# Output projection of a hybrid attention layer: eight column-and-token products replaced by seven half-size products

## The chip, the cores and the metric

The kernel runs on one core of a Trainium2 chip. The time is device microseconds of one execution; before the change it is 531.4 us (median of three runs, 531.16 to 531.54). Lower is better.

## The reference

One layer takes `x` (1024 tokens by 1024 features, float32), normalises it, projects it with `w_in`, runs two groups of attention heads, gates both, and projects the concatenated mix back:

```
h = rmsnorm(x, pre_g);  p = h @ w_in
ya = sliding_window_sink_attention(...) * silu(ag)     # 512 mix features
yb = differential_attention(...) * silu(bg)            # 512 mix features
y = concat([ya, yb]) @ w_out                           # (1024 x 1024) @ (1024 x 1024)
return x + rmsnorm(y, post_g)
```

The change concerns the product with `w_out` and what surrounds it. The norm after it is over a whole row of 1024 columns: a token's scale is known only when all of its columns are.

## The kernel before

The engines are programmed by hand, each with its own instruction list, and they meet only in semaphores. One list of steps, `SCHEDULE`, is built by `make_schedule()`; every engine walks it and issues its own part of each step, so the order of steps sets the order on every engine.

A float32 product is made at full matmul rate by splitting both operands into a high part in the fp32r format and a low part, the rest; three products high-high, low-high and high-low (`PASSES`) are added up in PSUM. ScalarE (ACT) makes a high part with a Copy; VectorE (DVE) or GpSimd (POOL) makes the low part with a subtraction of two SBUF tensors.

The input projection goes in 21 units (`UNITS`) of two halves, cut into six pieces of 4 matmuls; the pieces are spread between the steps of attention. The last five units are gates: ACT takes a tanh of PSUM (L775), DVE multiplies with PSUM (L973) and then with the head's output (L980), which lies in `qT_A` for group A and `out_B` for group B. After the last attention block some 20 pieces remain, and between them the steps `split_out` (wo_hi on ACT L744, wo_lo on POOL L660 for even k and DVE L984 for odd k) and `y_split` stand. SyncE issues the loads of `w_out` row block by row block (L584) into freed buffers.

The output projection runs over eight tiles of 128 tokens (t) and two column halves. One (t, half) is 24 matmuls of 128x512 (8 blocks of k in 3 passes, L1263) into one of four PSUM banks in `scores`. After it ACT squares the bank with a row sum (L851), DVE weights it with post_g (L1087), and when both halves of a tile are done DVE adds the sums (L1084), POOL takes the power -0.5 (L626), DVE scales and adds x (L1094, two instructions), and ACT issues the two stores (L858). The y parts of tile t+2 are split (ACT L841, DVE L1071) while tile t is multiplied. Each tile so finishes behind its own matmuls.

## Time and profile before

| | |
|---|---|
| median of 3 runs | 531.4 us |
| span of the profiled execution | 529.6 us |
| median minus span | 1.8 us |
| PE busy | 511.7 us, 97% |
| DVE, ACT, POOL busy | 269.9, 250.5, 105.8 us |
| output projection, from first matmul to the last | 436.25 to 523.97 us |
| from there to the end of the span | 5.6 us |

The span counts from the first to the last instruction of one execution. The profile gives no total of its own for that execution; the median is 1.8 us above its span. PE matmul spans overlap each other in the profile, so the distance between the starts of two rows, and not their lengths, gives the pace of the matmuls.

### The profile page before, as it was taken

How to read it: one execution, taken by the hardware profiler on the slowest of the kernel's cores; microseconds unless marked ns; L12 is line 12 of the kernel's file. 1: busy time of each engine (PE TensorE's matmuls, PEld its weight loads, DVE VectorE, ACT ScalarE, POOL GpSimd, SP SyncE). 2: the span in 40 equal slices, each digit the busy share in tenths (PEclk: the TensorE clock that was granted, in tenths of full speed). 3: DMA queues.
4: the chain of work that ended last, by engine and by line, in shares of the span. 5: the costliest groups of instructions: out<-in, count | busy, mean ns of one | idle time of the engine just before them, and what ended most of it. 6: DMA issues, size and time to landing. Idle time of an engine off the chain costs nothing.

```text
span 529.6 us, 7514 instructions
## 1 busy us (share of the span) xinstructions
PE 511.7 (97%) x2776; PEld 424.8 (80%) x2776; DVE 269.9 (51%) x650; ACT 250.5 (47%) x614; POOL 105.8 (20%) x91
## 2 busy tenths in 40 slices
...
GB/s 295 228 123 2 1 15 143 41 74 6 40 10 33 40 41 0 41 40 9 34 41 27 14 41 1 40 41 41 0 1 0 144 176 120 102 132 84 80 79 79
DMA packets 41300, 32.57 MB, mean 61 GB/s; under 512 B 18544, under 2 KB 35888, under 8 KB 41264
## 3 DMA queue, kind: packets, MB, share of 16 engines
...
q14 instruction: 14, 0.11, 0.1%
HBM read 27.40 MB, written 4.19 MB: 60 GB/s over the span
## 4 chain that ended last, share of the span: by engine, by line
PE 85%; ACT 4%; DVE 4%; issue 3%; DMA 2%; POOL 2%; SPq 0%; DVEq 0%; POOLq 0%; ACTq 0%
PE proj L1164 39%; PE scores L1263 14%; PE proj L1134 10%; PE scores L1183 7%; PE banks L1204 6%; PE banks L1194 3%; PE scores L1228 2%; PE banks L1246 2%; PE banks L1236 1%; PE scores L1107 1%; DVE k_stack L961 1%; DMA pre_g<-in_pre_norm_g 1%; DMA w_raw<-in_w_in 1%; ACT k_stack L762 1%; PE banks L1213 1%
## 5 line engine op out<-in xcount | busy, mean ns | idle before, releaser
L1164 PE MATMUL proj<-hT_hi,w_hi 128*128 128x512 f32 x336 | 90.0, 401 | 0.8 <-DVE k_stack L961 0.6
L1164 PE MATMUL proj<-hT_lo,w_hi 128*128 128x512 f32 x336 | 90.6, 402 | 0.0
L622 POOL TENSOR_TENSOR w_lo<-w_raw,w_hi 128x1024 fp32r<-128x1024 f32 x21 | 51.0, 2430 | 195.4 <-ACT w_hi L711 195.4
L1164 PE MATMUL proj<-hT_hi,w_lo 128*128 128x512 f32 x336 | 89.2, 400 | 0.0
L1164 PEld LDWEIGHTS proj<-hT_hi,w_hi 128*128 128x128 f32 x336 | 60.3, 188 | 15.0 <-issue 1.9
L1164 PEld LDWEIGHTS proj<-hT_hi,w_lo 128*128 128x128 f32 x336 | 60.8, 188 | 13.7 <-issue 1.9
L1164 PEld LDWEIGHTS proj<-hT_lo,w_hi 128*128 128x128 f32 x336 | 59.9, 188 | 13.2 <-issue 1.9
L1016 DVE CUSTOM_DVE_ANT_0 weights<-scores,dist_b 128x128 f32<-128x128 f32 (+7 forms) x64 | 45.9, 755 | 47.2 <-PE scores L1183 47.0
L782 ACT ACTIVATE weights<-weights,small 128x128 f32<-128x128 f32 (+7 forms) x64 | 49.0, 767 | 14.0 <-DVE small L1016 14.0
L792 ACT ACTIVATE weightsT<-banks 128x512 f32<-128x512 f32 (+3 forms) x48 | 23.5, 490 | 51.4 <-PE banks L1194 51.4
L1183 PE MATMUL scores<-k_stack,q_stack 128*128 128x512 f32 (+3 forms) x192 | 41.9, 353 | 0.0
L1204 PEld LDWEIGHTS banks<-v_sb,weightsT 128*128 128x128 f32 x288 | 36.3, 191 | 5.8 <-ACT weightsT L792 3.2
L1204 PE MATMUL banks<-v_sb,weightsT 128*128 128x128 f32 x288 | 37.8, 276 | 1.1 <-ACT weightsT L792 1.1
L1183 PEld LDWEIGHTS scores<-k_stack,q_stack 128*128 128x128 f32 x192 | 31.9, 189 | 4.8 <-DVE k_stack L961 0.4
L1000 DVE SCALAR_TENSOR_TENSOR weights<-weights,small,weights 128x512 f32<-128x512 f32 (+3 forms) x48 | 34.4, 745 | 1.1
L851 ACT ACTIVATE banks<-scores 128x512 f32<-128x512 f32 x16 | 9.3, 582 | 53.3 <-PE scores L1263 53.3
L626 POOL TENSOR_TENSOR small<-small 128x1 f32<-128x1 f32 (+1 forms) x24 | 16.9, 704 | 82.7 <-DVE small L1084 81.4
L1263 PE MATMUL scores<-wo_hi,hT_hi 128*128 128x512 f32 x128 | 32.0, 391 | 0.1
L820 ACT ACTIVATE a_weights<-a_weights,small 128x128 f32<-128x128 f32 x64 | 24.9, 391 | 14.7 <-DVE small L1044 14.6
L1263 PE MATMUL scores<-wo_hi,hT_lo 128*128 128x512 f32 x128 | 31.6, 389 | 0.0
L1263 PE MATMUL scores<-wo_lo,hT_hi 128*128 128x512 f32 x128 | 31.6, 389 | 0.0
L961 DVE TENSOR_TENSOR k_stack<-proj,k_stack 64x512 fp32r<-64x512 f32 x32 | 22.0, 688 | 15.6 <-ACT k_stack L762 14.8
...
## 6 DMA issues: line engine op xcount, KB each, us to landing
...
```

Source lines behind the costliest of these rows:

```text
L622: nc.gpsimd.tensor_tensor(w_lo[:, n % SPLIT], w_raw[:, n % RAW], w_hi[:, n % SPLIT].bitcast(F32), ALU.subtract).then_inc(w_lo_ready, 1)
L782: nc.scalar.activation(w, w, ACT.Exp, scale=-1.0, bias=min_b[:, 2 * u + m:2 * u + m + 1], accum_out=sum_b[:, 2 * u + m:2 * u + m + 1]).the ...
L792: nc.scalar.activation(weightsT[:, 4 * r:4 * r + blocks, :], turned[:, 0:P * blocks].rearrange("p (b q) -> p b q", q=P), ACT.Copy).then_in ...
L820: nc.scalar.activation(w, w, ACT.Exp, scale=-1.0, bias=min_a[:, s + j:s + j + 1], accum_out=sum_a[:, s + j:s + j + 1]).then_inc(a_exped, 1)
L961: nc.vector.tensor_tensor(k_lo[part, m, tokens], source[own, :], k_hi[own, m, tokens].bitcast(F32), ALU.subtract).then_inc(stack_lo, 1)
L1000: nc.vector.scalar_tensor_tensor(w0, w1, mix_b[:, u:u + 1], w0, ALU.mult, ALU.add).then_inc(b_mixed, 1)
L1016: nc.vector.tensor_tensor_reduce(out=weights_1[:, 0:keys] if m else weights_0[:, u % 2, 0:keys], in0=scores[:, 1024 * m:1024 * m + keys], ...
L1134: last = nc.tensor.matmul(proj[:, n % 2, 0:VG], h[:, k, tokens], w[:, k, cols], start=(p == 0 and k == 0), stop=(p == PASSES - 1 and k == ...
L1164: last = nc.tensor.matmul(to, w[:, slot, k, :], h[:, k, HALF * half:HALF * half + HALF], start=(p == 0 and k == first), stop=(p == PIECES ...
L1183: last = nc.tensor.matmul(scores[:, 1024 * m + first:1024 * m + first + width], q_stack[head][m][:, P * block_:P * block_ + P], k[:, m, fi ...
L1204: last = nc.tensor.matmul(mixed[:, P * (u % 4):P * (u % 4) + P], weightsT[:, b, :], v_sb[:, b, P * head:P * head + P], start=(b == 0), sto ...
L1263: last = nc.tensor.matmul(scores[:, at:at + HALF], y[:, k, tokens], w[:, k, cols], start=(p == 0 and k == 0), stop=(p == PASSES - 1 and k ...
```

## The change

The 1024x1024x1024 product is cut into halves of tokens, of mix features and of columns: y = [A1 B1; A2 B2] (tokens 0 to 511 and 512 to 1023; group A and group B features) and w_out = [W00 W01; W10 W11]. Instead of eight half-size products, seven are made, each 512 tokens by 512 features by 512 columns, that is four PSUM banks of 12 matmuls of 128x512 (4 blocks of k in 3 passes): 48 matmuls. Their operands and results:

- T1 = W01-W00, T2 = W11-T1, T4 = W10-T2, T3 = W11-W01 on POOL (step `wo_sums`), 2048 elements per partition each; S1 = A2+B2, S2 = S1-A1, S3 = A1-A2, S4 = B1-S2 on DVE (`y_sum`), two instructions of 1024 elements each.
- in this order: P1 = A1·W00 and P2 = B1·W10, P6 = S2·T2, P7 = S3·T3, P5 = S1·T1, P3 = S4·W11, P4 = B2·T4. P6, P7 and P4 go on top of P1 in the four banks of `scores`; P2 has the two `banks` and the two `proj`, and then P5 starts there and P3 goes on top.
- running sums are taken out between products: ACT copies `scores` after P1, P6 and P7 (`u_copied`), DVE adds the other four banks to these copies after P2, P5 and P3 (`c_added`). Each next product waits in each bank for the copy or add of that bank.

All operands are split again into high and low parts: ACT makes wo_hi (2048 elements in one instruction) and y_hi (two of 1024) for every product, DVE makes y_lo (two of 1024) for every product and wo_lo for P1 and P2, POOL makes wo_lo for the other five. They live in three sets of buffers (`OUT_SLOTS`), so product i waits with its splits for the end of product i-3. `w_out` is loaded as a whole, 4 MB, into one buffer when the last attention product is done.

Squares of each half row (ACT) follow the adds. The rest of the tiles' ends, for all eight tiles, now stands in DVE's list behind the adds of P3, that is behind everything else, and all stores stand in ACT's list behind the last squares.

The core of the diff (declarations, index functions, buffer places left out; P1 ... P4 are numbers 0 to 6 in the order P1, P2, P6, P7, P5, P3, P4):

```diff
-    for t in range(TILES):
-        if t + 2 < TILES:
-            steps.append(("y_split", t + 2))
-        steps += [("out_project", t, 0), ("out_project", t, 1), ("post", t)]
+        if len(pieces) - at == WO_HIGH_AT:
+            steps.append(("wo_split", P1))
+        if len(pieces) - at == 9:
+            steps.append(("y_split", P1))
+    steps += [("y_split", P2), ("wo_split", P2), ("wo_sums",)]
+    steps += [("out_product", P1), ("y_sum", SUM_S1), ("y_sum", SUM_S2), ("y_split", P6), ("wo_split", P6)]
+    steps += [("out_product", P2), ("y_sum", SUM_S3), ("y_split", P7), ("wo_split", P7)]
+    steps += [("out_product", P6), ("y_sum", SUM_S4), ("y_split", P5), ("wo_split", P5)]
+    steps += [("out_product", P7), ("y_split", P3), ("wo_split", P3)]
+    steps += [("out_product", P5), ("y_split", P4), ("wo_split", P4)]
+    steps += [("out_product", P3), ("out_product", P4)]
...
+            sp.wait_ge(b_valued, B_UNITS)
+            for side in range(2):
+                rows = w_out[0, A_PAIRS * HEAD_DIM * side:A_PAIRS * HEAD_DIM * (side + 1), :]
+                sp.dma_start(wo_raw[HEAD_DIM * side:HEAD_DIM * (side + 1), 0:HALF_K, :],
+                             rows.rearrange("(k p) d -> p k d", p=HEAD_DIM)).then_inc(wo_loaded[0], 16)
+            for k, head in enumerate(B_ORDER):
+                sp.dma_start(wo_raw[:, HALF_K + k, :],
+                             w_out[0, A_WIDTH + P * head:A_WIDTH + P * head + P, :]).then_inc(wo_loaded[1], 16)
...
+                elif step == "wo_sums":
+                    pool.wait_ge(wo_loaded[1], 64)
+                    pool.wait_ge(wo_lo_ready, P1 + 1)
+                    nc.gpsimd.tensor_tensor(wo_part(0, 0), wo_part(0, 1), wo_part(0, 0),
+                                            ALU.subtract).then_inc(wo_summed, 1)
+                    pool.wait_ge(w_lo_ready, NU)
+                    pool.wait_ge(projected, 2 * NU)
+                    pool.wait_ge(wo_summed, DIF_T1)
+                    nc.gpsimd.tensor_tensor(t2[:, :, :], wo_part(1, 1), wo_part(0, 0),
+                                            ALU.subtract).then_inc(wo_summed, 1)
+                    pool.wait_ge(wo_summed, DIF_T2)
+                    pool.wait_ge(wo_lo_ready, P2 + 1)
+                    nc.gpsimd.tensor_tensor(wo_part(1, 0), wo_part(1, 0), t2[:, :, :],
+                                            ALU.subtract).then_inc(wo_summed, 1)
+                    nc.gpsimd.tensor_tensor(wo_part(0, 1), wo_part(1, 1), wo_part(0, 1),
+                                            ALU.subtract).then_inc(wo_summed, 1)
+                elif step == "wo_split" and i[0] > P2:
+                    n = i[0]
+                    pool.wait_ge(wo_hi_ready, n + 1)
+                    nc.gpsimd.tensor_tensor(wo_lo[n % OUT_SLOTS][:, :, :], wo_operand(n),
+                                            wo_hi[n % OUT_SLOTS][:, :, :].bitcast(F32),
+                                            ALU.subtract).then_inc(wo_lo_ready, 1)
...
+                    elif n == P4:
+                        dve.wait_ge(post_g_loaded, 16)
+                        low, high = slice(0, HALF), slice(HALF, D_MODEL)
+                        for t in range(TILES):
+                            early, late = ((0, low), (1, high)) if t < PAIRS else ((1, high), (0, low))
+                            for half, cols in (early, late):
+                                dve.wait_ge(y_squared, squares_done(t, half))
+                                if half == late[0]:
+                                    nc.vector.scalar_tensor_tensor(
+                                        y_mean[:, t:t + 1], y_square[:, 2 * t:2 * t + 1], EPS,
+                                        y_square[:, 2 * t + 1:2 * t + 2], ALU.add, ALU.add).then_inc(y_meaned, 1)
+                                c = c_half(t, half)
+                                weighted = c11[:, t % PAIRS, :] if t >= PAIRS and half == 0 else c
+                                if t >= PAIRS and half == 0:
+                                    dve.wait_ge(y_added, 2 * (t - PAIRS) + 2)
+                                nc.vector.tensor_tensor(weighted, c, post_g[:, cols],
+                                                        ALU.mult).then_inc(y_weighted, 1)
+                            dve.wait_ge(y_weighted, 2 * t + 2)
+                            dve.wait_ge(res_loaded[t], 16)
+                            dve.wait_ge(y_rooted, t + 1)
...
+                elif step == "out_product":
+                    n = i[0]
+                    slot = n % OUT_SLOTS
+                    for r in range(PAIRS):
...
+                        elif n in (P6, P7, P4):
+                            pe.wait_ge(u_copied, PAIRS * {P6: 0, P7: 1, P4: 2}[n] + r + 1)
...
+                        for p, (y, w) in enumerate(((y_hi, wo_hi), (y_lo, wo_hi), (y_hi, wo_lo))):
+                            if r == 0 and p == 0:
+                                pe.wait_ge(wo_hi_ready, n + 1)
+                            if r == 0 and p == 2:
+                                pe.wait_ge(wo_lo_ready, n + 1)
```

How instructions stand on POOL before, from the first split of `w_out` to the last root (`wo_lo` is the low part of the weights, `small` a tile's column sum):

```order
L660 TENSOR_TENSOR wo_lo<-wo_early,wo_hi 128x1024
L660 TENSOR_TENSOR wo_lo<-w_raw,wo_hi 128x1024
L660 TENSOR_TENSOR wo_lo<-wo_early,wo_hi 128x1024
L660 TENSOR_TENSOR wo_lo<-w_raw,wo_hi 128x1024
L626 TENSOR_TENSOR small<-small 128x1 x8
```

POOL's part is over before the first tile's end; behind it stand only the roots.

The same place on POOL in the changed kernel (`wo_raw` is all of w_out, `t_101` is T2, `wo_lo_90` to `92` are the low parts in the three buffer sets):

```order
L714 TENSOR_TENSOR wo_raw<-wo_raw 128x4x512
L719 TENSOR_TENSOR t_101<-wo_raw 128x2048
L723 TENSOR_TENSOR wo_raw<-wo_raw,t_101 128x4x512
L725 TENSOR_TENSOR wo_raw<-wo_raw 128x4x512
L730 TENSOR_TENSOR wo_lo_92<-t_101,wo_hi_89 128x2048
L730 TENSOR_TENSOR wo_lo_90<-wo_raw,wo_hi_87 128x2048
L730 TENSOR_TENSOR wo_lo_91<-wo_raw,wo_hi_88 128x2048
L730 TENSOR_TENSOR wo_lo_92<-wo_raw,wo_hi_89 128x2048
L730 TENSOR_TENSOR wo_lo_90<-wo_raw,wo_hi_87 128x2048
L679 TENSOR_TENSOR small<-small 128x1 x8
```

Four instructions of 1024 elements have become nine of 2048, the four sums in front of the first wo_lo.

DVE before, at the start of the output projection (`hT_lo` is the low part of y, `hT_hi` the high part; `y_out` is a tile's weighted result):

```order
L973 SCALAR_TENSOR_TENSOR gate<-gate,proj 128x512
L980 TENSOR_TENSOR out_B<-gate,out_B 128x512
L1071 TENSOR_TENSOR hT_lo<-qT_A,hT_hi 128x2x128 x2
L1071 TENSOR_TENSOR hT_lo<-out_B,hT_hi 128x4x128
L1087 TENSOR_TENSOR y_out<-scores,post_g 128x512
L1084 SCALAR_TENSOR_TENSOR small<-small 128x1
L1087 TENSOR_TENSOR y_out<-scores,post_g 128x512
L1094 SCALAR_TENSOR_TENSOR y_out<-y_out,small,x_res 128x512 x2
```

The split of the next tile, two or three instructions of at most 512 elements, stands in front of the end of the current one; each tile repeats that.

DVE in the changed kernel at the same place, from the last gate's product to the splits for P7 (`s_99` is S1, `s_100` S2, `y_lo_96` to `98` low parts of y, `c_103` the sums of tokens 0 to 511, columns 0 to 511):

```order
L1073 SCALAR_TENSOR_TENSOR gate<-gate,proj 128x512
L1080 TENSOR_TENSOR out_B<-gate,out_B 128x512
L1171 TENSOR_TENSOR y_lo_97<-out_B,y_hi_94 128x1024 x2
L1084 TENSOR_TENSOR wo_lo_91<-wo_raw,wo_hi_88 128x2048
L1184 TENSOR_TENSOR s_99<-qT_A,out_B 128x1024 x2
L1188 TENSOR_TENSOR s_100<-s_99,qT_A 128x1024 x2
L1171 TENSOR_TENSOR y_lo_98<-s_100,y_hi_95 128x1024 x2
L1203 TENSOR_TENSOR c_103<-banks,c_103 128x512 x2
L1203 TENSOR_TENSOR c_103<-proj,c_103 128x512 x2
L1191 TENSOR_TENSOR qT_A<-qT_A 128x2x8x64 x2
L1171 TENSOR_TENSOR y_lo_96<-qT_A,y_hi_93 128x1024 x2
```

The end of a tile no longer stands between the splits; sums and splits of two SBUF tensors stand in a row there.

DVE in the changed kernel behind the adds of P3 (`c_102` are the sums of tokens 0 to 511, columns 512 to 1023; `x_res` a tile of x, which becomes the output):

```order
L1203 TENSOR_TENSOR c_102<-banks,c_102 128x512 x2
L1203 TENSOR_TENSOR c_102<-proj,c_102 128x512 x2
L1219 TENSOR_TENSOR c_103<-c_103,post_g 128x512
L1212 SCALAR_TENSOR_TENSOR small<-small 128x1
L1219 TENSOR_TENSOR c_102<-c_102,post_g 128x512
L1226 SCALAR_TENSOR_TENSOR x_res_107<-c_103,small,x_res_107 128x512
L1226 SCALAR_TENSOR_TENSOR x_res_107<-c_102,small,x_res_107 128x512
```

Before, such a group of five stood behind each tile's matmuls; now the eight groups stand in a row, of which the first is shown.

## Rows read from the trace of the kernel before

**Rows 1.** The page: busy time of each engine.

```profile
span 529.6 us, 7514 instructions
...
PE 511.7 (97%) x2776; PEld 424.8 (80%) x2776; DVE 269.9 (51%) x650; ACT 250.5 (47%) x614; POOL 105.8 (20%) x91
```

**Rows 2.** The chain that ended last, from 380 us: start, length, engine, tile, line.

```profile
409.55 1.87 PE banks L1204 x16
...
438.20 74.90 PE scores L1263 x329
```

**Rows 3.** Timeline of PE, output projection: start, length, engine, line, operation.

```profile
436.25 2.45 PE L1263 MATMUL scores<-wo_hi,hT_hi 128*128 128x512 f32 x8
438.53 2.01 PE L1263 MATMUL scores<-wo_hi,hT_lo 128*128 128x512 f32 x8
440.38 1.98 PE L1263 MATMUL scores<-wo_lo,hT_hi 128*128 128x512 f32 x8
...
521.99 1.98 PE L1263 MATMUL scores<-wo_lo,hT_hi 128*128 128x512 f32 x8
```

**Rows 4.** Timeline of all engines, the last tile.

```profile
519.35 0.69 DVE L1087 TENSOR_TENSOR y_out<-scores,post_g 128x512 f32<-128x512 f32 x1 [3.17 <-ACT banks L851]
...
524.00 0.58 ACT L851 ACTIVATE banks<-scores 128x512 f32<-128x512 f32 x1 [4.75 <-PE scores L1263]
524.49 0.19 ACT L851 ACTIVATION_READ_ACCUMULATOR banks<-scores 128x1 f32 x1
524.72 0.16 DVE L1084 SCALAR_TENSOR_TENSOR small<-small 128x1 f32<-128x1 f32 x1 [4.68 <-ACT banks L851]
524.80 0.68 DVE L1087 TENSOR_TENSOR y_out<-scores,post_g 128x512 f32<-128x512 f32 x1
524.96 0.55 POOL L626 TENSOR_TENSOR small<-small 128x1 f32<-128x1 f32 x1 [10.33 <-DVE small L1084]
525.64 1.41 DVE L1094 SCALAR_TENSOR_TENSOR y_out<-y_out,small,x_res 128x512 f32<-128x512 f32 x2 [0.16 <-POOL small L626]
526.42 1.00 ACTq L858 DMA_DIRECT2D out<-y_out  x2
```

**Rows 5.** Timeline, 418 to 445 us: ACT, POOL and DVE split weights.

```profile
420.62 2.00 ACT L744 ACTIVATE wo_hi<-wo_early 128x1024 fp32r<-128x1024 f32 x2
...
425.57 0.60 ACT L775 ACTIVATE gate<-proj 128x512 f32<-128x512 f32 x1 [2.94 <-PE proj L1164]
...
427.19 2.69 POOL L660 TENSOR_TENSOR wo_lo<-w_raw,wo_hi 128x1024 fp32r<-128x1024 f32 x1 [2.75 <-ACT wo_hi L744]
...
428.09 2.87 DVE L984 TENSOR_TENSOR wo_lo<-w_raw,wo_hi 128x1024 fp32r<-128x1024 f32 x1 [0.48 <-ACT wo_hi L744]
...
429.84 3.38 POOL L660 TENSOR_TENSOR wo_lo<-wo_early,wo_hi 128x1024 fp32r<-128x1024 f32 x1
...
431.01 0.60 ACT L775 ACTIVATE gate<-proj 128x512 f32<-128x512 f32 x1 [2.00 <-PE proj L1164]
...
433.69 1.21 DVE L984 TENSOR_TENSOR wo_lo<-wo_early,wo_hi 128x1024 fp32r<-128x1024 f32 x1
...
437.28 2.45 POOL L660 TENSOR_TENSOR wo_lo<-w_raw,wo_hi 128x1024 fp32r<-128x1024 f32 x1 [4.06 <-ACT wo_hi L744]
```

**Rows 6.** Timeline, 110 to 118 us: DVE reading PSUM beside POOL.

```profile
113.76 2.39 POOL L622 TENSOR_TENSOR w_lo<-w_raw,w_hi 128x1024 fp32r<-128x1024 f32 x1 [4.83 <-ACT w_hi L711]
113.85 1.41 DVE L956 SCALAR_TENSOR_TENSOR q_stack<-proj,q_stack 64x512 fp32r<-64x512 f32 x2
```

**Rows 7.** Timeline of the DMA queue of SyncE, loads of w_out.

```profile
414.21 2.45 SPq L584 DMA_DIRECT2D wo_early<-in_w_out  x4
416.78 2.78 SPq L584 DMA_DIRECT2D w_raw<-in_w_out  x4
```

**Rows 8.** Stretches: us, busy of PE, PEld, DVE, ACT, POOL, clock, DMA share, GB/s.

```profile
415.00:420.00 5.00, 5.00 (x26) 4.12 (x25) 1.96 (x3) 0.69 (x1) 0.00 (x0) 1.00 0.93 206
420.00:430.00 10.00, 10.00 (x46) 8.29 (x45) 7.53 (x6) 5.94 (x7) 5.50 (x3) 1.00 0.79 212
```

**Rows 9.** Stretches after the last matmul (PEclk is the granted clock).

```profile
524.00:526.00 2.00, 0.00 (x0) 0.00 (x0) 1.12 (x3) 0.69 (x2) 0.55 (x1) 1.00 0.00 0
526.00:527.00 1.00, 0.00 (x0) 0.00 (x0) 1.00 (x2) 0.00 (x0) 0.00 (x0) 0.72 0.00 0
527.00:528.00 1.00, 0.00 (x0) 0.00 (x0) 0.05 (x1) 0.00 (x0) 0.00 (x0) 0.50 0.74 272
```

**Rows 10.** Timeline of PE at the start.

```profile
1.54 5.38 PE L1140 MATMUL proj<-ident 128*128 128x128 f32 x24 [1.54 <-POOL ident L631]
...
18.39 1.06 PE L1107 MATMUL scores<-ident,x_in 128*128 128x128 f32 x8 [1.00 <-DVE x_in L869]
```

**Rows 11.** Groups by shape, POOL: busy, mean ns, idle before.

```profile
L622 POOL TENSOR_TENSOR w_lo<-w_raw,w_hi 128x1024 fp32r<-128x1024 f32 x21 | 51.0, 2430 | 195.4 <-ACT w_hi L711 195.4
...
L643 POOL TENSOR_TENSOR wv_lo<-wv_raw,wv_hi 128x1280 fp32r<-128x1280 f32 x1 | 2.9, 2927 | 3.7 <-ACT wv_hi L686 3.7
```

**Rows 12.** Groups by shape, ACT.

```profile
L792 ACT ACTIVATE weightsT<-banks 128x512 f32<-128x512 f32 x24 | 14.3, 596 | 21.6 <-PE banks L1194 21.6
...
L744 ACT ACTIVATE wo_hi<-wo_early 128x1024 fp32r<-128x1024 f32 x4 | 4.1, 1054 | 0.0
```

More of the change, by code:

```diff
@@ L76 @@
 WV_AT = 5
-Y_PARTS = 3
-WO_RAW = 4
-OLDEST = NU % SPLIT
 FIRST_PIECES = 24
+PAIRS = TILES // 2
+HALF_K = KT // 2
+PRODUCTS = 7
+P1, P2, P6, P7, P5, P3, P4 = range(PRODUCTS)
+Y_ORIGINALS = {P1: (0, 0), P2: (1, 0), P4: (1, 1)}
+SUM_S1, SUM_S2, SUM_S3, SUM_S4 = range(1, 5)
+DIF_T1, DIF_T2, DIF_T4, DIF_T3 = range(1, 5)
+OUT_SLOTS = 3
 B_UNITS = B_HEADS * TILES
@@ L202, in make_schedule @@
         take(max(0, count))
-    last = (NU - 1) * 2 * PIECES
-    outs = list(range(KT))
     while at < len(pieces):
@@ L275, in hybrid_layer @@
     lam_in = place("lam_in", 118, [P, 4, HEAD_DIM])
-    wo_hi = place("wo_hi", 96, [P, KT, D_MODEL], F32R)
-    wo_lo = place("wo_lo", 128, [P, KT, D_MODEL], F32R)
-    wo_early = place("wo_early", 72, [P, 2 * SPLIT, D_MODEL])
-    post_g = place("post_g", 201.75, [P, D_MODEL])
-    x_res = place("x_res", 76, [P, 2, D_MODEL])
-    y_out = place("y_out", 88, [P, 2, D_MODEL])
+    wo_raw = place("wo_raw", 96, [P, KT, D_MODEL])
+    out_slots = [128, 0, 32]
+    wo_hi = [place(f"wo_hi{i}", at, [P, HALF_K, HALF], F32R) for i, at in enumerate(out_slots)]
+    wo_lo = [place(f"wo_lo{i}", at + 8, [P, HALF_K, HALF], F32R) for i, at in enumerate(out_slots)]
+    y_hi = [place(f"y_hi{i}", at + 16, [P, HALF_K, HALF], F32R) for i, at in enumerate(out_slots)]
+    y_lo = [place(f"y_lo{i}", at + 24, [P, HALF_K, HALF], F32R) for i, at in enumerate(out_slots)]
+    s1 = place("s1", 64, [P, HALF_K, HALF])
+    s2 = place("s2", 72, [P, HALF_K, HALF])
+    t2 = place("t2", 80, [P, HALF_K, HALF])
+    c12 = place("c12", 80, [P, PAIRS, HALF])
+    c11 = place("c11", 88, [P, PAIRS, HALF])
+    c22_parts = [place("c22_low", 180.25, [P, 2, HALF]), place("c22_high", 188.25, [P, 2, HALF])]
+    post_g = place("post_g", 160.25, [P, D_MODEL])
+    x_res = [place(f"x_res{t}", (64 if t < PAIRS else 96) + 4 * (t % PAIRS), [P, D_MODEL]) for t in range(TILES)]
     taken = [0]
@@ L328, in hybrid_layer @@
     mixed = banks[:, 512:1024]
+    out_x = [scores[:, HALF * r:HALF * r + HALF] for r in range(PAIRS)]
+    out_y = [turned, mixed, proj[:, 0, :], proj[:, 1, :]]
     def sem(name):
@@ L335, in hybrid_layer @@
     w_loaded = [sem(f"w_loaded{i}") for i in range(RAW)]
-    wo_loaded = [sem(f"wo_loaded{i}") for i in range(WO_RAW)]
+    wo_loaded = [sem("wo_loaded0"), sem("wo_loaded1")]
     pre_g_loaded = sem("pre_g_loaded")
@@ L340, in hybrid_layer @@
     v_shifted = sem("v_shifted")
-    res_loaded = [sem("res_loaded0"), sem("res_loaded1")]
-    stored = [sem("stored0"), sem("stored1")]
+    res_loaded = [sem(f"res_loaded{t}") for t in range(TILES)]
+    stored = sem("stored")
     ident_made = sem("ident_made")
@@ new lines, in heads_b, with half_rows, y_operand @@
+    def heads_b(half, r):
+        tokens = out_B[:, 2 * r:2 * r + 2, HALF * half:HALF * half + HALF]
+        return tokens.rearrange("p s (c q) -> p s c q", q=CHUNK)
+    def half_rows(to, r):
+        return to[:, 2 * r:2 * r + 2, :].rearrange("p s (c q) -> p s c q", q=CHUNK)
+    def y_operand(i, r):
+        if i in Y_ORIGINALS:
+            side, half = Y_ORIGINALS[i]
+            return heads_b(half, r) if side else heads_a(half, r)
+        if i == P7:
+            return heads_a(1, r)
+        return half_rows(s1 if i == P5 else s2, r)
@@ new lines, in wo_part, with wo_operand, c22, c_half @@
+    def wo_part(rows, cols):
+        return wo_raw[:, HALF_K * rows:HALF_K * (rows + 1), HALF * cols:HALF * cols + HALF]
+    def wo_operand(i):
+        if i == P6:
+            return t2[:, :, :]
+        return wo_part(*{P1: (0, 0), P2: (1, 0), P7: (0, 1), P5: (0, 0), P3: (1, 1), P4: (1, 0)}[i])
+    def c22(r):
+        return c22_parts[r // 2][:, r % 2, :]
+    def c_half(t, half):
+        r = t % PAIRS
+        if t < PAIRS:
+            return (c12 if half else c11)[:, r, :]
+        return c22(r) if half else out_x[r]
```

306 lines of the change are left out of this document (167 added, 139 removed).

## The prediction

> **What bounds the kernel now.** I read the page first: PE is busy 97% of a span of 529.6 us, every other engine half of it or less [rows 1]. Then the chain of waits: its last long piece is 74.9 us of output-projection matmuls in one run [rows 2]. The PE timeline gives their pace: groups of 8 start at 440.38 and, 45 groups later, at 521.99, so one matmul takes 81.61/360 = 0.2267 us. The first two groups start 2.28 and 1.85 us after one another's beginning instead of 1.81: some 0.5 us is lost at the start [rows 3]. Last I read the end: the last product ends at 523.97, ACT squares, DVE sums and weights, POOL makes the root, DVE scales, the stores go out, and the span ends 5.6 us after PE [rows 4]. PE sets the time, and a tile's end is hidden behind the next tile's matmuls for all tiles but one.
>
> The span is 1.8 us below the median of the runs. I sum over the span and add 1.8 at the end.
>
> **Matmuls.** 16 groups of 24, or 384, become 7 x 4 x 12 = 336. 48 x 0.2267 = 10.9 us go. The operands of P1 are ready early: ACT's wo_hi starts behind the gate of 425.57 [rows 5], y_hi is done near 430.2, DVE's low parts near 432.9, and PE needs them at 436.25. So the 0.5 us goes too: -11.4 us. Copies and adds that free a bank have a product's time, 10.9 us, for four of about 0.6 to 0.7 us [rows 4, 12]: nothing, as long as their engines are not late.
>
> **The tiles' ends.** DVE gets all eight behind the adds of P3. One costs 0.69 for the first weighting, then from 524.72 to 527.05 for sum, second weighting, root and two scalings [rows 4]: 3.02 us, eight are 24.2 us. From the end of P3 it takes 0.04 + 0.7 (its last add) + 24.2 to the last scaling, and the stores another 2.55 (527.05 to 529.6) [rows 1, 4]. In tiles 0 to 3 the second weighting now reads two SBUF tensors and POOL's root may stand behind it (below): 0 to 0.45 us each, I take half, 0.9 in all. That is 28.4 us from the end of P3. P4 lies beside the first 10.9 of them, 17.5 are left after PE. Before, 5.6: +11.9 us. ACT's twelve later squares at 0.77 [rows 4] and the x loads lie beside this. The tail alone eats what the matmuls give.
>
> **The port between DVE and POOL.** The rows show one rule. A POOL instruction of 427.19 ends at 429.88; DVE's of 428.09 ends at 430.96, 1.08 later; POOL's next, issued at 429.84, ends at 433.22, 2.26 after DVE; alone they take 1.21 and 2.43 [rows 5, 11]. So they ran in turns, neither beside the other, and the one that waited went first, even between two POOL instructions in a row. DVE's with one operand in PSUM ran 1.41 for two beside POOL, undisturbed [rows 6]. The Trainium skill, SBUF — State Buffer, "Who interferes with whom", has this as a rule that speaks against the change: a DVE instruction with two SBUF inputs contends with a GpSimd instruction that reads SBUF, and the one that issues second blocks fully. By that rule, the trace agrees, the 11.3 us below are owed; without it the sum would be that of rival 1.
>
> The change puts nine 2048-element instructions on POOL where four of 1024 stood, beside sums and splits of two SBUF tensors on DVE. Their price: POOL 2.43 + 2.27 = 4.7 us (from 1024 to 1280 elements it rose 0.5 us, which would give 4.4; twice 2.43 gives 4.86) [rows 11]. The Trainium skill, GPSIMD Engine Reference, "Elementwise — side-by-side cycle accounting", states 4497 ns for this size; no row here has it, and by that figure the wait below would be about 0.8 us shorter. DVE 1.2 for 1024, 2.3 for 2048 [rows 5]. ACT 1.05 for 1024, 1.95 for 2048 (+0.9 per 1024 by 596 against 1054) [rows 12].
>
> The list, step by step. The last attention product ends at 411.42 [rows 2]; w_out's 4.19 MB flow at 206 to 268 GB/s (212 at a share of 0.79) [rows 8], so the rows of P1 are in by about 423 and all by 429 to 434, with the 2 us that issues take [rows 7]. T1 starts near 432 and runs to 437.4 (behind one DVE instruction), and the last but one gate product on DVE waits for it; T2 follows to 442.5, and the last gate product waits too. y_lo of P2 twice and wo_lo of P2 then end at 447.8; PE wants wo_lo of P2 at 447.1 + 1.8 = 448.9: hidden with 1 us to spare. From there it isn't. POOL has T4 (it waits for wo_lo of P2) and T3, DVE has S1, S1, S2, S2, and they take turns: S1 449.0, T4 453.6, S1 454.6, T3 459.2, S2 460.3, S2 461.5. Behind S2 stands ACT with y_hi of P6 (463.6) and, in its list behind that, wo_hi of P6 (465.6), though T2 was ready long before. PE ends P2 at 458.0 and waits 7.6 us. POOL makes wo_lo of P6 from 465.6 to 470.3; PE's third pass is there at 467.4 and waits 3.0. For P7 the same pair costs 0.7, since S3 stands behind POOL too. P5, P3 and P4 find their operands ready: the work per product there is one POOL instruction and at most six on DVE in 10.9 us. Sum of the waits: +11.3 us.
>
> **The clock.** PE idle from 523.97 had its full 2.4 GHz until 526 and half of it in the slices from 526 and 527 (0.72, 0.50) [rows 9]. At the start 24 small transposes took 5.38 us, 0.22 each, later 8 took 1.06, about 0.13 [rows 10]. So after 7.6 us without work P6 starts at 1.2 GHz. Half of some 6 us, 3.0, is the upper end; zero if it comes back while PE waits for wo_lo. The first 8 matmuls at half speed end just before 470.3 and are free; I take 1.2.
>
> Sum: 529.6 - 11.4 + 11.9 + 11.3 + 1.2 = 542.6 us of span; with 1.8, **544.4 us**, 2.4% slower.
>
> **Bounds.** POOL's size: four of its instructions stand on the way to P6, -1.2 to +0.6. Clock -1.2 to +1.8. Root -0.9 to +0.9. Loads: if all of w_out is in only at 438, +4. Turns: if DVE kept the port through its row of four, S2 would be done by 452.6, but T4, T3 and wo_lo then follow in a row and P6 still gets its low part near 469: about the same.
>
> **Rivals.** 1. No turn is lost at the port, DVE and POOL run beside each other. For: in all of the run before the port cost the path nothing one can see. Against: the three pairs in rows 5. Then POOL needs five times 4.7 from 432, is done with wo_lo of P6 at 455.5, before 459.8, and PE never waits: 529.6 - 11.4 + 11.0 (no root wait) = 529.2, with 1.8 531.0, no difference.
> 2. Faster, by the length of a tile's end on DVE. With the port free the time is 531.0 + 8 x (t - 3.02) for t us a tile, and it is faster by 0.2% from t below 2.94. It could be 2.7, 528.4 us, if DVE overlapped its instructions where no sum or root is fresh (the squares of tiles 0 to 3 are old when it starts). Against: 2.33 of the 3.02 are one chain in rows 4, which the new list keeps whole for each tile, and rows 5 say that the port isn't free.
> 3. The port costs only part (an ACT list that gets y_hi of P6 out early, or smaller POOL instructions): half of 11.3, 537 to 538.
> 4. It costs more: w_out late, waits at P2 too, half clock through P6 and again at P7: 549 to 555. For: PE has 1 us of slack at P2.
>
> **How the numbers follow.** Forecast 0.68, rival 1 0.08, rival 2 0.04, rival 3 0.09, rival 4 0.11. The forecast's own bounds give 541 to 549. The range of 8 in 10 takes a part of rivals 3 and 4: 538 to 551. What a measurement can tell from no change is 0.2%, 530.3 to 532.5. Faster: rival 2 and a quarter of rival 1, which a little rounding carries below 530.3: 0.06. Same: most of the rest of rival 1, 0.05. Slower 0.89.
>
> **What would show it.** In the profile after: PE groups at the same 0.2267; gaps before the first matmul of P6 of 7 to 8 us, after a group of 8 in it some 3 us, near 0.7 in P7, none before P5, P3, P4; DVE S1 and S2 rows of 5.6 us in place of 1.2, beside POOL's of 4.7; a granted clock under 1 around 460 to 470 us; and behind the last matmul a row of DVE instructions of 15 us with PE idle. I am wrong if DVE's two-SBUF instructions keep 1.2 us beside POOL, if PE's end is before 515, or if DVE's last scaling comes under 10 us after PE's end.

## The result and the profile after

The changed kernel takes 542.77 us (median of 4 runs, 542.50 to 544.03), the kernel before on the same chip 531.44: ratio 1.0216, 95% interval 1.0202 to 1.0229. 544.4 us was forecast, 1.6 us or 0.3% too much. The profiled execution of the changed kernel was its slowest, 544.03 us; a later series of the same kernel, whose profiled execution took 542.43 us, serves beside it below and is called the second profile.

The page of the changed kernel: span, busy time of PE, DVE and POOL, PE in 40 slices and its granted clock.

```profile
span 542.2 us, 7425 instructions
PE 504.8 (93%) x2728; PEld 418.4 (77%) x2728; DVE 312.5 (58%) x658; ACT 266.2 (49%) x615; POOL 141.1 (26%) x96
PE   6899999999999999999898999999999997599970
PEclk9999999999999999999999999999999999599995
```

PE had 511.7 us to do over 529.6 and has 504.8 over 542.2 [rows 1]: it has less work and more idle time. The holes stand in two places, slices 34 and 35 (about 447 to 474 us) and the last two. In slice 35 and in the last one the granted clock is 0.5, half of full speed.

PE's timeline in the output projection (start, duration, groups of matmuls; the brackets tell the idle time before and what ended it): the first group, the first of P6, its second and third pass, and the last of the program.

```profile
436.13 1.07 PE L1409 MATMUL scores<-wo_hi,y_hi 128*128 128x512 f32 x4
465.92 2.05 PE L1409 MATMUL scores<-wo_hi,y_hi 128*128 128x512 f32 x4 [7.84 <-ACT wo_hi L819]
470.51 2.07 PE L1409 MATMUL scores<-wo_lo,y_hi 128*128 128x512 f32 x4 [0.84 <-POOL wo_lo L730]
524.50 1.07 PE L1409 MATMUL scores<-wo_lo,y_hi 128*128 128x512 f32 x4
```

P1 starts where the first tile did [rows 3]. P1 and P2 are 96 matmuls of 0.2267 us and end at 457.9; P6 starts at 465.92, 8.0 us later. The third pass stands 4.59 us behind it, where 8 matmuls at full clock take 1.81. Here they ran at half clock, 3.7 us, and then PE waited the rest for POOL's low part; at full clock the wait would be 2.8.

What stood in front of P6 on DVE, POOL and ACT (three views, DVE's from 430 us on):

```profile
430.10 6.76 DVE L1171 TENSOR_TENSOR y_lo<-qT_A,y_hi 128x1024 fp32r<-128x1024 f32 x2
437.49 4.39 DVE L1080 TENSOR_TENSOR out_B<-gate,out_B 128x512 f32<-128x512 f32 x1
448.52 6.75 DVE L1184 TENSOR_TENSOR s<-qT_A,out_B 128x1024 f32<-128x1024 f32 x2
455.20 6.72 DVE L1188 TENSOR_TENSOR s<-s,qT_A 128x1024 f32<-128x1024 f32 x2
```
```profile
448.75 5.45 POOL L723 TENSOR_TENSOR wo_raw<-wo_raw,t 128x2048 f32<-128x2048 f32 x1 [7.41 <-DVE wo_lo L1084]
454.16 5.54 POOL L725 TENSOR_TENSOR wo_raw<-wo_raw 128x2048 f32<-128x2048 f32 x1
465.89 4.56 POOL L730 TENSOR_TENSOR wo_lo<-t,wo_hi 128x2048 fp32r<-128x2048 f32 x1 [6.19 <-ACT wo_hi L819]
```
```profile
462.01 2.00 ACT L918 ACTIVATE y_hi<-s 128x1024 fp32r<-128x1024 f32 x2 [13.79 <-DVE s L1188]
463.92 1.89 ACT L819 ACTIVATE wo_hi<-t 128x2048 fp32r<-128x2048 f32 x1
```

S1 and S2, two instructions of 1.2 us each, took 6.75 and 6.72 where 2.4 would do; T4 and T3 stood beside them at 5.45 and 5.54, where one that nothing disturbs (wo_lo of P6) takes 4.56. A blocked instruction is drawn longer, not as idle time. The same happened earlier: T1 (430.32 to 435.77) held y_lo of P1, T2 (436.43 to 441.34) a gate product of 0.69 us, drawn as 4.39. ACT had been idle for 13.8 us, waiting for S2, with wo_hi of P6 behind y_hi in its list.

The end, all engines, behind the last matmul, which ends at 525.57: the root of tile 3, the first weightings of tiles 4 and 5, then of tile 7 the second weighting, the root and the two scalings.

```profile
525.88 0.93 POOL L679 TENSOR_TENSOR small<-small 128x1 f32<-128x1 f32 x1 [2.30 <-DVE small L1212]
528.27 0.69 DVE L1219 TENSOR_TENSOR c_low<-c_low,post_g 128x512 f32<-128x512 f32 x1
531.12 0.68 DVE L1219 TENSOR_TENSOR c_low<-c_low,post_g 128x512 f32<-128x512 f32 x1
537.48 0.68 DVE L1219 TENSOR_TENSOR c<-scores,post_g 128x512 f32<-128x512 f32 x1
537.64 0.55 POOL L679 TENSOR_TENSOR small<-small 128x1 f32<-128x1 f32 x1 [2.30 <-DVE small L1212]
538.33 0.75 DVE L1226 SCALAR_TENSOR_TENSOR x_res<-c,small,x_res 128x512 f32<-128x512 f32 x1 [0.16 <-POOL small L679]
539.00 0.75 DVE L1226 SCALAR_TENSOR_TENSOR x_res<-c_high,small,x_res 128x512 f32<-128x512 f32 x1
```

PE ends at 525.57, DVE's last scaling at 539.75, the span at 542.2: 16.6 us behind PE, where the kernel before had 5.6 [rows 4].

### The profile page after: what moved, and what is told of

It reads as the page before. It is cut to its first block, busy times and chain, and to the rows that moved or that the text cites. A ratio compares the mean times of both kernels' runs of the same rounds, so it can differ in the third digit from the quotient of the medians.

```text
span 542.2 us, 7425 instructions
## 1 busy us (share of the span) xinstructions
PE 504.8 (93%) x2728; PEld 418.4 (77%) x2728; DVE 312.5 (58%) x658; ACT 266.2 (49%) x615; POOL 141.1 (26%) x96
## 4 chain that ended last, share of the span: by engine, by line
PE 76%; DVE 10%; ACT 4%; POOL 3%; issue 3%; DMA 2%; SPq 0%; DVEq 0%; POOLq 0%; ACTq 0%
PE proj L1296 37%; PE proj L1266 10%; PE scores L1315 6%; PE banks L1336 6%; PE scores L1409 4%; PE banks L1326 3%; PE proj L1409 2%; PE banks L1409 2%; DVE x_res L1226 2%; PE scores L1360 2%; PE banks L1378 2%; DVE s L1184 1%; DVE s L1188 1%; POOL small L679 1%; PE banks L1368 1%
## 5 line engine op out<-in xcount | busy, mean ns | idle before, releaser
L1145 DVE CUSTOM_DVE_ANT_0 a_weights<-scores,dist_a,small 128x128 f32<-128x128 f32 x64 | 22.5, 407 | 13.6 <-PE scores L1360 13.5
L747 POOL TENSOR_TENSOR a_weights<-a_weights,small 128x512 f32<-128x512 f32 x16 | 16.6, 1041 | 39.2 <-DVE small L1159 39.2
L1409 PE MATMUL scores<-wo_hi,y_hi 128*128 128x512 f32 x64 | 18.9, 421 | 7.8 <-ACT wo_hi L819 7.8
L1326 PE MATMUL banks<-ident,weights 128*128 128x128 f32 x144 | 23.8, 274 | 2.3 <-ACT weightsT L868 1.6
L851 ACT ACTIVATE gate<-proj 128x512 f32<-128x512 f32 x16 | 9.5, 592 | 33.3 <-PE proj L1296 22.8
```

The lines of the kernel that those rows point to most:

```text
L1326: last = nc.tensor.transpose(turned[:, P * (b - 4 * r):P * (b - 4 * r) + P], weights_0[:, u % 2, P * b:P * b + P], ident[:, :])
L1409: last = nc.tensor.matmul(to, y[slot][:, k, P * r:P * r + P], w[slot][:, k, :], start=(starts and p == 0 and k == 0), stop=(p == PASSES - ...
```

## Why it came so: two costs, four terms

My theory after this comparison is the prediction's: the tile ends behind the last product, and turns at the port that DVE and POOL share, each cost about what the matmuls give. Against it stand three rivals: that something else about the new sums holds P6 up (ACT's list, the loads, DVE's load as such); that a long tail is owed to the eight ends as such and can't be moved; and that half clock is a third cost of its own.

### The port: take POOL's sums away

```diff
-  nc.gpsimd.tensor_tensor(wo_part(0, 0), wo_part(0, 1), wo_part(0, 0), ALU.subtract)
+  nc.gpsimd.tensor_tensor(wo_part(0, 0)[:, :, 0:8], wo_part(0, 1)[:, :, 0:8], wo_part(0, 0)[:, :, 0:8], ALU.subtract)
```

(the same for T2, T4 and T3; P6 takes W11 as its second operand. The kernel leaves out nearly all of the four sums.)

> The four sums of w_out on POOL compute 8 of each 512 columns, and P6 takes W11 for T2: the kernel leaves out nearly all of T1 to T4. Theory (POOL's long instructions hold the port, and DVE's sums of two SBUF tensors wait for them): DVE's S1 and S2 take about 1.2 us each, P6 and P7 start on time, the granted clock stays full, the whole 13.1 us before P4's end come back: 529.7 us. Rival (the wait before P6 is the length of ACT's and DVE's own lists, without the port): DVE and ACT do the same work, so most of the 8 us before P6 stays: about 538.

531.37 us (10 runs, 530.89 to 531.64), ratio to before 0.9993 (0.9983 to 1.0002). DVE's rows of S1 and S2 and, later, of S4 in this kernel:

```profile
443.04 2.41 DVE L1184 TENSOR_TENSOR s<-qT_A,out_B 128x1024 f32<-128x1024 f32 x2
445.37 2.41 DVE L1188 TENSOR_TENSOR s<-s,qT_A 128x1024 f32<-128x1024 f32 x2
464.68 6.77 DVE L1194 TENSOR_TENSOR s<-out_B,s 128x1024 f32<-128x1024 f32 x2
```

S1 and S2 are back at 1.2 each, PE's timeline has no gap from P1 to the last product, and 11.4 us come back; the tail is still 16.7. The rival's 538 is out. The 529.7 that I gave was 1.7 too low: it counted the 13.1 us between P2 and P4 of the first profile, with its half clock (below). The time is near that of the prediction's rival 1, 531.0. S1 also starts 5.5 us earlier than in the changed kernel (443.04 against 448.52), since T1 and T2 no longer hold DVE before it. S4 beside POOL's wo_lo of P7 still took 6.77 in this kernel: the port goes on costing, but there it lies behind PE's work. This kernel takes two causes away at once, POOL's time for the sums and the turns; the next one parts them.

### The port: take away only DVE's second operand in SBUF

```diff
+  dve.wait_ge(u_copied, PAIRS)
-  nc.vector.tensor_tensor(half_rows(s1, r), heads_a(1, r), heads_b(1, r), ALU.add)
+  nc.vector.tensor_tensor(half_rows(s1, r), psum_rows(r), heads_b(1, r), ALU.add)
-  nc.vector.tensor_tensor(half_rows(s2, r), half_rows(s1, r), heads_a(0, r), ALU.subtract)
+  nc.vector.tensor_tensor(half_rows(s2, r), psum_rows(r), heads_a(0, r), ALU.subtract)
```

> S1 and S2 on DVE read their first operand from PSUM (the bank of P1) in place of SBUF, so the sums are of other data; sizes, order and all of POOL's work stay, and DVE waits in addition for ACT's copies of P1. Theory (only a DVE instruction with two SBUF operands is kept out by POOL): S1 and S2 take 1.2 us each beside T4 and T3, S2 is done near 453.5, P6 starts on time, and then waits some 5 us for its second y_lo (which has two SBUF operands and stands behind T3 and wo_lo of P6), and P7 some 3 us: 3 to 4 us less than the changed kernel in all, about 539.3 us. Rival (POOL slows every DVE instruction, or DVE's time is its own): no change, 542.8.

539.29 us (538.92 to 539.69), ratio 1.0144 (1.0129 to 1.0159), 3.5 us under the changed kernel. DVE from S1 to y_lo of P6, and POOL beside it:

```profile
448.84 2.35 DVE L1189 TENSOR_TENSOR s<-scores,out_B 128x1024 f32<-128x1024 f32 x2
451.11 2.35 DVE L1193 TENSOR_TENSOR s<-scores,qT_A 128x1024 f32<-128x1024 f32 x2
454.64 10.18 DVE L1175 TENSOR_TENSOR y_lo<-s,y_hi 128x1024 fp32r<-128x1024 f32 x2 [1.19 <-ACT y_hi L922]
```
```profile
449.07 4.63 POOL L727 TENSOR_TENSOR wo_raw<-wo_raw,t 128x2048 f32<-128x2048 f32 x1 [7.41 <-DVE wo_lo L1088]
453.66 4.62 POOL L729 TENSOR_TENSOR wo_raw<-wo_raw 128x2048 f32<-128x2048 f32 x1
458.25 5.49 POOL L734 TENSOR_TENSOR wo_lo<-t,wo_hi 128x2048 fp32r<-128x2048 f32 x1
```

With one operand in PSUM the same sums take 1.2 us each beside POOL's T4, and T4 takes 4.63: neither feels the other. The Trainium skill, SBUF — State Buffer, "Who interferes with whom", says that a DVE instruction with at most one SBUF input, outside the 2-port perf modes, does not contend with GpSimd; by that rule, the trace agrees. The next pair with two operands in SBUF, y_lo of P6, pays instead: 10.18 us for two, the first behind T3, the second behind wo_lo of P6. On PE:

```profile
459.42 0.73 PE L1414 MATMUL scores<-wo_hi,y_lo 128*128 128x512 f32 x2
464.88 1.22 PE L1414 MATMUL scores<-wo_hi,y_lo 128*128 128x512 f32 x2 [4.72 <-DVE y_lo L1175]
```

P6 starts without a wait, and 5.0 us go in its second pass (two matmuls from 459.42 end their turn at 459.87, the next start at 464.88), where the changed kernel waits 8.0 and 2.8. With 0.3 us for the first y_lo and 0.8 before P7's third pass, the waits are 6.1 us against 11.1. That they did not bring 5.0 us but 3.5 is half clock behind the pause: the 18 matmuls from 464.88 took 5.7 us instead of 4.1. I had expected some 3 us before P7 and no half clock; the two misses cancel, and the total of 539.3 came out partly by luck. What was forecast for the rows themselves came: 1.2 us each for S1 and S2, and a wait of 5 us for the second y_lo. So the loss follows the pair of operands, not the amount of work, and the rival is out.

### ACT's list: wo_hi of P6 first

```diff
-  ("y_sum", SUM_S2), ("y_split", P6), ("wo_split", P6)]
+  ("y_sum", SUM_S2), ("wo_split", P6), ("y_split", P6)]
```

> ACT makes wo_hi of P6 before y_hi of P6, so that it does not wait for S2. Theory (turns at the port): POOL's wo_lo of P6 then asks for the port while S2 still waits, goes between S2's two instructions, and S2 ends 5 us later: PE waits 9 to 10 us before P6 and about 1 in it, P7's wait grows to some 3: 544 us, slower by 1 to 2 us though the operand is ready earlier. Rival (the order of ACT's list costs the 2.8 us inside P6): they go, 540.

544.59 us (544.38 to 544.77), ratio 1.0242 (1.0225 to 1.0259), 1.8 us over the changed kernel. DVE's S2, the third of POOL's instructions in a row, PE's first group of P6 and its sixth, and the clock (0.50) from 470 to 474:

```profile
455.87 11.02 DVE L1188 TENSOR_TENSOR s<-s,qT_A 128x1024 f32<-128x1024 f32 x2
```
```profile
460.33 5.47 POOL L730 TENSOR_TENSOR wo_lo<-t,wo_hi 128x2048 fp32r<-128x2048 f32 x1
```
```profile
468.18 2.08 PE L1409 MATMUL scores<-wo_hi,y_hi 128*128 128x512 f32 x4 [9.44 <-ACT y_hi L918]
475.60 1.08 PE L1409 MATMUL scores<-wo_lo,y_hi 128*128 128x512 f32 x4
```
```profile
470.00:474.00 4.00, 4.00 (x11) 3.07 (x10) 4.00 (x7) 0.00 (x0) 0.00 (x0) 0.50 0.00 0
```

Bringing wo_hi forward let POOL put a third instruction, wo_lo of P6, in a row behind T4 and T3. S2's second half then stood behind that too: 11.02 us for the two against 6.72. P6 starts 9.6 us late, though its third pass no longer waits. The number of POOL instructions that get in beside DVE's row sets the price: 4.3 us for this one, and (6.75 + 6.72 - 4.8) / 2 = 4.3 for each of the two in the changed kernel. That price is what my theory had said. The total is not the port's alone. P6 starts 1.6 us later than in the changed kernel, and its third pass saves the 2.8 us of waiting: these two would make this kernel faster. What made it slower is half clock, with no wait left to hide in: the first 20 matmuls of P6 took 7.4 us (468.18 to 475.60) where full clock takes 4.5. Another 0.5 us stands ahead of P1, which starts at 436.80 here. I had named about 1 us in P6 and some 3 before P7, where 0 and 0.5 came, and no half clock; the 544 came out by luck. The rival's 2.8 us did go, but its 540 counted neither the later start nor the clock.

### The tail: tile ends earlier

```diff
-  steps += [("out_product", P6), ("y_sum", SUM_S4), ...
+  steps += [("out_product", P6), ("squares", 0), ("y_sum", SUM_S4), ...
+  steps += [("weigh", 0), ("out_product", P7), ...
+  ... ("wo_split", P4), ("squares", 1), ("weigh", 1)]
...
   # DVE, behind each add of P3
+  if n == P3:
+      if r:
+          finish(r - 1)      # two scalings of tile r-1
+      weigh_late(r)          # sum and second weighting of tile r
...
+  sp.dma_start(out[0, P * t:P * t + P, cols], x_res[t][:, cols])   # was ACT's
```

> The waits before P6 stay; the ends of the tiles are moved: the squares and weightings of the halves that are final early go into idle time of DVE, the ends of tiles 0 to 3 go between the adds of P3, and SyncE issues the stores. Theory (the tail behind PE is DVE's list of eight ends, 24 us from P3's end): PE's end stays at 525.6, the last scaling comes near 533 in place of 539.7, total 536. Rival (the tail is the stores' list on ACT or the DMA): the same 16.6 us behind PE as long as the bytes are the same, 541 to 543.

535.3 us (535.16 to 537.3), ratio 1.0078 (1.006 to 1.0096), 7.5 us under the changed kernel. The last group on PE, the last scaling, and P6's first group:

```profile
523.13 1.07 PE L1420 MATMUL scores<-wo_lo,y_hi 128*128 128x512 f32 x4
530.24 0.74 DVE L1030 SCALAR_TENSOR_TENSOR x_res<-c_high,small,x_res 128x512 f32<-128x512 f32 x1
```
```profile
466.21 2.04 PE L1420 MATMUL scores<-wo_hi,y_hi 128*128 128x512 f32 x4 [7.84 <-ACT wo_hi L824]
```

PE ends at 524.20, the span at 533.4: 9.2 us behind PE instead of 16.6, and the pause before P6 is what it was. The stores moved too, from ACT's queue to SyncE's, but they take the same 2.4 us behind the last scaling as before (530.98 to 533.4; 539.75 to 542.2). All of the 7.4 us lies ahead of the last scaling, so the rival of the stores' list is out: the tail was a matter of where the tile ends stood in DVE's list, and 7.4 of its 11.0 us could be had by moving them.

### Half clock: fill PE's pauses

```diff
+  if n == P6:                      # before its first pass; 12 more before its third
+      for _ in range(32):
+          nc.tensor.matmul(out_x[3], zeros[:, 0:P], zeros[:, :], start=False, stop=True)
```

> The changed kernel with 44 more matmuls of a tile of zeros on PE (32 of 128x512 between P2 and P6, 12 before P6's third pass, all added to the bank of P6's fourth column group, so the sums stay what they are). They fill the time in which PE has no operands. My theory: half clock after PE's pause cost 2.3 us (16 matmuls from 470.51 took 5.93 us instead of 3.63); with PE busy the granted clock stays near 1.00 between 458 and 476 and this comes back: 540.5 us against 542.8, the waits for operands themselves (8.0 and 2.8 us) stay. Rival: the stretch was slow for another cause (reads of operands while the other engines write), or the fillers themselves hold P6 up: 542.8 or more.

543.31 us (543.25 to 543.33), ratio 1.0222 (1.0207 to 1.0237): nothing came back. The clock did as told, 1.00 in all slices from 456 to 486, and PE's way from P6's first group to the last group took 56.9 us (466.84 to 523.78) instead of 58.6 (465.92 to 524.50). But P6 itself came 0.56 us later after P1 than in the changed kernel. Most of that was my own doing: ACT made the tile of zeros in front of wo_hi of P1, 0.52 us, and DVE's whole row of instructions moved by it. What was left did not explain why the median should not fall, unless the changed kernel's median had hardly any half clock in it. That called for a second look at the changed kernel and a cleaner filler.

> The changed kernel itself, unaltered, beside the next kernel on the same chip. Its first profiled run took 544.03 us, its other three 542.50 to 542.84. My theory: where the two pauses lie is fixed, how long half clock lasts behind them is not. PE's way from the first matmul of P6 to the last group took 58.58 us in the profile of 544.03 us and 56.92 us in the kernel of the tail with the same pauses; so I expect a median of 542.6 us, and if this profile is one of about 542.6, some 57.0 to 57.5 us for that way and fewer slices at 0.50. Rival: the way is 58.6 us again, and half clock costs some 2 us in every run; the 1.3 us between the runs came from before the output projection.

542.46 us (542.43 to 542.48), ratio 1.0204 (1.019 to 1.0218). The second profile's P6, and the clock in windows (start and end, length, busy time of PE, PEld, DVE, ACT, POOL, then the granted clock), first of the changed kernel's first profile, then of the second:

```profile
466.03 2.04 PE L1409 MATMUL scores<-wo_hi,y_hi 128*128 128x512 f32 x4 [7.85 <-ACT wo_hi L819]
470.61 1.19 PE L1409 MATMUL scores<-wo_lo,y_hi 128*128 128x512 f32 x4 [0.83 <-POOL wo_lo L730]
481.97 1.20 PE L1409 MATMUL scores<-wo_lo,y_hi 128*128 128x512 f32 x4 [0.19 <-POOL wo_lo L730]
522.90 1.07 PE L1409 MATMUL scores<-wo_lo,y_hi 128*128 128x512 f32 x4
```
```profile
460.00:462.00 2.00, 0.00 (x0) 0.00 (x0) 1.92 (x2) 0.00 (x0) 0.00 (x0) 0.88 0.00 0
470.00:472.00 2.00, 1.49 (x4) 1.20 (x5) 2.00 (x2) 0.00 (x0) 0.46 (x1) 0.50 0.00 0
474.00:476.00 2.00, 2.00 (x8) 1.55 (x7) 2.00 (x2) 2.00 (x2) 0.00 (x0) 0.70 0.00 0
```
```profile
462.00:464.00 2.00, 0.00 (x0) 0.00 (x0) 0.82 (x2) 1.87 (x2) 0.00 (x0) 0.84 0.01 4
468.00:470.00 2.00, 1.78 (x5) 0.86 (x3) 2.00 (x1) 0.00 (x0) 2.00 (x1) 0.50 0.00 0
470.00:472.00 2.00, 1.39 (x6) 1.17 (x7) 2.00 (x2) 0.00 (x0) 0.56 (x1) 0.96 0.00 0
```

PE does the same at the same instants in both: last matmul near 458, first of P6 at 465.9 and 466.0, the third pass at 470.5 and 470.6. The clock is granted differently. In the first profile it falls within 460 to 462 and is whole again only behind 475; in the second it falls within 462 to 464 and is back at 470. In the second, then, half clock covers only the first 8 matmuls, which end before POOL's wo_lo is there: it costs nothing. The first group behind a wait takes 0.12 to 0.13 us more than the others in this profile, behind P7's wait too, where the clock is 1.00. PE's way took 56.9 us (466.03 to 522.90), so the first profile's 58.6 had 1.7 us of half clock net (2.3 in 16 matmuls, less 0.35 of waiting before P7's third pass, since P7 came later, and less the two slower groups). The program is the same in both; what decides between them no run shows. 7 of the 8 runs of the changed kernel took 542.43 to 542.84. That these had the short half clock is inferred from their times: only one of them was profiled, and the mean granted clock does not tell them apart (0.973 to 0.982, against 0.976 in the run of 544.03).

> The kernel of the fillers (44 matmuls of a tile of zeros while PE waits), but with the tile of zeros made by ACT before y_hi of P6, where ACT is idle, instead of before wo_hi of P1, where its 0.52 us stood ahead of DVE's whole row. My theory: 543.31 us of the first fillers were 0.5 us of that and 0.1 us of the fillers' own end, and half clock costs the median of the changed kernel only 0.3 us: 542.4 to 542.8 us, 0 to 0.3 us under the changed kernel on the same chip. Rival: half clock costs 2 us in the median too, and this kernel gets them back: 540.8 us.

542.78 us (542.54 to 543.06), ratio 1.0211 (1.0197 to 1.0225), 0.3 over the changed kernel beside it. The time is in the 542.4 to 542.8 that I gave, but over the changed kernel where I had said at or under it; P6 came 29.82 us after P1 against 29.77, and P1 itself 0.24 us later (436.50 against 436.26). PE's way took 56.95 us (466.32 to 523.27) at full clock, against 56.87 in the second profile. The rival's 540.8 is out. A clock kept whole is worth nothing in the median here, because a wait for POOL already covers the half clock; in the kernels with P6's operands read from PSUM and with wo_hi first nothing covered it, and it cost 1.5 and 2.8 us.

### A version that avoids both: sums on DVE, then with the early tile ends

```diff
-  ... ("wo_split", P2), ("wo_sums",)]
+  steps += [("wo_sum", DIF_T2), ("y_split", P2), ("wo_split", P2), ("wo_split", P6)]
+  steps += [("out_product", P1), ("y_sum", SUM_S1), ("y_sum", SUM_S2), ("y_split", P6), ("wo_sum", DIF_T4)]
+  steps += [("out_product", P2), ("wo_sum", DIF_T3), ("y_sum", SUM_S3), ("y_split", P7), ("wo_split", P7)]
...
-  nc.gpsimd.tensor_tensor(t2[:, :, :], wo_part(1, 1), wo_part(0, 0), ALU.subtract)
+  nc.vector.tensor_tensor(t2[:, :, :], wo_part(1, 1), wo_part(0, 0), ALU.subtract)
...
-  elif step == "wo_split" and i[0] > P2:        # POOL
+  elif step == "wo_split" and i[0] >= P3:
```

> The changed kernel with the four sums of w_out and the low parts of five of the seven products on DVE, which has them behind one another with its own sums; POOL keeps only the low parts for P3 and P4, beside which DVE has no instruction with two SBUF operands but adds from PSUM. ACT's low-part source of P6 early; each half of y_hi is waited for on its own. The order of products and the end are as in the changed kernel. My theory: no instruction stands behind the other engine's, a sum is 2.3 us on DVE instead of 4.7 on POOL, PE waits about 1.2 us before P7 and nowhere else, clock 1.00: 542.8 - 11.0 - 2.3 + 1.2 = 530.7 us, the same as before the change. Rival: DVE has too much to do in the order in which it stands, and P6 or P2 waits for it by 5 us or more: over 536.

531.23 us (10 runs, 531.02 to 531.72), ratio 0.9994 (0.9984 to 1.0003). ACT now also waits for each half of an operand sum by itself. Two of its rows on DVE, T2 and S2:

```profile
438.41 2.29 DVE L1076 TENSOR_TENSOR t<-wo_raw 128x2048 f32<-128x2048 f32 x1
449.56 2.36 DVE L1192 TENSOR_TENSOR s<-s,qT_A 128x1024 f32<-128x1024 f32 x2
```

DVE makes a sum of 2048 elements in 2.29 us where POOL took 4.6 to 5.5, its own sums keep 1.2, and PE has no gap at all from 436.25 to 512.57; even the 1.2 us that I had expected before P7 did not appear. The window of P1 and P2 (busy time of PE, PEld, DVE, ACT, POOL):

```profile
436.00:458.00 22.00, 22.00 (x98) 18.21 (x97) 21.12 (x18) 10.50 (x11) 0.00 (x0) 1.00 0.00 1
```

DVE is busy 21.12 of 22 us, and that is enough. DVE had room for POOL's share of the work, though not for POOL beside it.

> The kernel of the sums on DVE together with the tile ends of the earlier experiment (squares and weightings early, the ends of tiles 0 to 3 between P3's adds, stores on SyncE's queue). My theory: the two costs are independent, so the gain of the tail (542.8 - 535.3 = 7.5 us) and the gain at the port (12.1 us) add: 523.2 us, faster than both kernels (531.4 and 542.8). Rival: the two do not add, since the tail's work on DVE now meets DVE's sums and splits: 527 to 531.

523.81 us (523.61 to 523.88), ratio 0.9855 (0.984 to 0.987): 1.4% faster than the kernel before and 19 us under the changed one. The end of it:

```profile
span 522.0 us, 7426 instructions
511.66 1.07 PE L1424 MATMUL scores<-wo_lo,y_hi 128*128 128x512 f32 x4
518.78 0.75 DVE L1014 SCALAR_TENSOR_TENSOR x_res<-c_high,small,x_res 128x512 f32<-128x512 f32 x1
```

PE ends at 512.73, the span 9.3 later. Of the changed kernel's 542.6 (between its two medians) the early tile ends take 7.4 and the port 11.4 (542.6 - 531.2): 523.8. The two add, as my theory had it (523.2 was forecast).

## Why the prediction was right, term by term

The forecast's span was 529.6 - 11.4 + 11.9 + 11.3 + 1.2 = 542.6. The spans measured were 542.2 and 540.6; the 1.8 us beside the span came out (544.03 - 542.2 and 542.43 - 540.6). The median of 542.77 therefore corresponds to a span of 541.0, and 1.6 us were too much. Against the second profile, by which the terms are measured here, it is 2.0: 529.6 - 11.4 + 11.1 (waits) + 11.0 (end) + 0 (clock) + 0.25 (the two slower groups behind the waits, which no term had) = 540.6. The mechanism was right in both large costs.

- **Matmuls, -11.4.** In the kernel without waits PE runs from 436.25 to 512.57; before, it ended at 523.97 [rows 3, 4] from the same start: -11.4.
- **Waits at the port, +11.3.** By the second profile: P2's end at 458.03 to 466.03, 8.0 (7.6 forecast); the third pass at 470.61 instead of 467.84, 2.8 (3.0); P7's third pass at 481.97 instead of 481.62, 0.35 (0.7). Together 11.1. The reading of three pairs in [rows 5] (turns; the one that waited goes first, even between two POOL instructions in a row) carried the whole list: S1, T4, S1, T3, S2, S2 came in that order, with one row of 5.6 us in each pair. S2 was done at 461.9 against 461.5 forecast. The kernel before never had this case in this length. Ahead of it the list was off: T1 came 1.7 us earlier and held y_lo of P1 (done at 436.86, not near 432.9; PE wants its second half at 437.5), T2 held the last but one gate product, and the last was not held at all. wo_lo of P2 was ready at 448.60 instead of 447.8. This late start and POOL's shorter instructions partly offset each other in the 8.0, and that neither product waited for these operands was a matter of 0.2 to 0.6 us.
- **POOL's size, 4.7.** Undisturbed it was 4.56 (wo_lo of P6) to 4.63 (T4 beside DVE's reads of PSUM). The Trainium skill, GPSIMD Engine Reference, "Elementwise — side-by-side cycle accounting", states 4497 ns: nearer than my 4.7, and 0.1 under what these traces show.
- **The tiles' ends, +11.9.** 11.0 came. The step that failed by 0.9 is "one costs 3.02". That was a sum of durations up to the end of the last scaling. In the trace after, DVE's next instruction starts 0.61 behind a weighting of 0.69, and 0.67 behind a scaling of 0.75, so the step from tile to tile is 2.85 (528.27 to 531.12 and on to 536.81), 0.17 less. The root's wait was 0.38 in tiles 0 to 3 (0.93 against 0.55), near the upper bound of 0.45, not half of it. 4 x 3.24 + 4 x 2.85 = 24.4 instead of 25.1; the rest is small change at the last add and the stores (2.45 for 2.55).
- **Clock, +1.2.** 0 in the second profile and 1.7 net in the first. Both lie in the bounds of 0 to 3.0; the lower end ("zero if it comes back while PE waits for wo_lo") is what the second profile shows and, by their times, most runs. I took a value between two cases; both profiles lie off it, and this term is the largest part of the 1.6 to 2.0 us too much.
- **Rivals.** Rival 1's time, 531.0, is near what the kernels without the long turns take, 531.37 and 531.23, but only the edits brought it. Rival 2's point was 2.94 us a tile: with the wait at the root the mean is 3.05, and 531.0 + 8 x 0.03 = 531.2 is what was measured. Rival 3 named y_hi of P6 out early, or smaller POOL instructions, and no run has either; wo_hi first is another edit (544.59), and DVE's operands in PSUM gave a partial cost by another way (539.29, its 537 to 538). Rival 4 was nearer than the 1 us of slack at P2 said: wo_lo of P2 was ready at 448.60, and PE wanted it at 448.8. PE's timeline shows no gap at P2.
